# Output weights as the last segment of a four-slot weight ring, and the order of the first output products and the broadcast rows, in a one-core diffusion block

## The reference

```python
p = u @ w_in                       # four branches (conformer, SSD, Hyena, short conv) and gates
merged = sum(gates[b] * (y[b] @ w_branch[b]) for b in "abcd")
mix_lat = merged @ w_out
h_lat = layer_norm(DN_ALPHA * h_lat + mod_lat[2] * mix_lat, ln_g[l, 0], ln_b[l, 0])
ffn_lat = moe_ffn(modulate(h_lat, mod_lat[3], mod_lat[4]), lp)   # h * (1 + scale) + shift
h_lat = layer_norm(DN_ALPHA * h_lat + mod_lat[5] * ffn_lat, ln_g[l, 1], ln_b[l, 1])
```

## Time and profile before

| | |
|---|---|
| median of three runs | 2642.73 us (2639.09 to 2645.9) |
| profiled execution, its own time | 2640.42 us |
| its span | 2638.4 us |
| PE busy | 2436.1 us, 92% |
| DVE busy | 1627.1 us, 62% |
| ACT busy | 941.0 us, 36% |
| PE's granted clock over the span | 0.962 of full speed |

### The profile page before, as it was taken

One profiled execution on the slowest core, in us unless ns is written; L12 is line 12 of the kernel. 1 busy time (PEld: TensorE's weight loads), 2 busy tenths in 40 slices (PEclk: granted clock), 3 DMA queues, 4 the chain that ended last, 5 costly groups with the idle time before them and its releaser, 6 DMA issues. The chain is left out here.

```text
span 2638.4 us, 30395 instructions
## 1 busy us (share of the span) xinstructions
PE 2436.1 (92%) x11864; PEld 1966.6 (75%) x11864; DVE 1627.1 (62%) x1628; ACT 941.0 (36%) x1090; POOL 293.3 (11%) x250
## 2 busy tenths in 40 slices
PE   7889989989997889999999999999499999999984
PEld 3337868768886788788877788878478888888871
DVE  4543359833330773632885635667688888888876
ACT  4132311133321343201111100021267778777763
POOL 3310000000001420000000000100012122121210
PEclk9899989999998999999999999999699999999997
DMA  4341135312323422211111113533579999999946
GB/s 174 129 153 39 42 124 188 136 57 72 114 99 121 128 80 68 96 48 46 48 41 48 40 48 118 202 148 126 239 268 363 368 360 364 365 370 388 386 171 255
DMA packets 95118, 437.49 MB, mean 166 GB/s; under 512 B 16056, under 2 KB 28616, under 8 KB 80298
## 3 DMA queue, kind: packets, MB, share of 16 engines
q1 hardware_dynamic: 68330, 357.81, 36.8%
q0 software_dynamic: 26688, 78.30, 8.5%
HBM read 401.51 MB, written 55.51 MB: 173 GB/s over the span
## 5 line engine op out<-in xcount | busy, mean ns | idle before, releaser
L390 PE MATMUL ps<-uT_upper_rest,ring_rest 128*128 128x512 f32 x1296 | 512.9, 396 | 0.0
L390 PE MATMUL ps<-uT_upper_rest,mix_upper 128*128 128x512 f32 x768 | 307.5, 400 | 9.6 <-DVE mix_val L2329 5.2
L390 PE MATMUL ps<-uT_rest,mix_upper 128*128 128x512 f32 x768 | 306.4, 399 | 0.0
L390 PEld LDWEIGHTS ps<-uT_upper_rest,ring_rest 128*128 128x128 f32 x1296 | 244.6, 189 | 62.2
L390 PEld LDWEIGHTS ps<-uT_upper_rest,mix_upper 128*128 128x128 f32 x768 | 145.5, 190 | 47.4 <-DVE mix_val L2329 5.7
L390 PEld LDWEIGHTS ps<-uT_rest,mix_upper 128*128 128x128 f32 x768 | 145.4, 189 | 33.1 <-issue 0.5
L1762 ACT ACTIVATE mix_gates<-ps 128x1024 f32<-128x1024 f32 x24 | 24.7, 1028 | 385.5 <-PE ps L390 369.0
L1813 DVE TENSOR_TENSOR mix_prod<-mix_gates,ps 128x1024 f32<-128x1024 f32 x24 | 29.3, 1221 | 213.0 <-PE ps L390 213.0
L2793 PE MATMUL ps<-ex_u_raw_rest,uT_rest 128*128 128x256 f32 x560 | 157.1, 281 | 0.0
L390 PE MATMUL ps<-uT_upper_rest,xbc_upper 128*128 128x512 f32 x336 | 136.2, 405 | 7.6 <-DVE ring_rest L819 7.6
L2791 PE MATMUL ps<-ring_rest,uT_rest 128*128 128x256 f32 (+1 forms) x416 | 135.0, 325 | 3.2 <-DVE uT_rest L3100 2.4
(11 more groups left out here) (454 smaller groups left out, 5613.5 us busy)
## 6 DMA issues: line engine op xcount, KB each, us to landing
sb_spare<-in_ex_g SPq DMA_DIRECT2D x35, 2048.0 KB
ex_u_raw<-in_ex_u SPq DMA_DIRECT2D x35, 2048.0 KB, 10.6
sb_merged<-in_ex_d SPq DMA_DIRECT2D x35, 2048.0 KB
ring<-in_conv SPq DMA_DIRECT2D x32, 512.0 KB, 3.3
ring<-in_w_gate SPq DMA_DIRECT2D x32, 512.0 KB, 3.3
mix_piece<-in_w_late POOLq DMA_DIRECT2D x32, 512.0 KB, 5.1
ring<-in_w_ssd SPq DMA_DIRECT2D x21, 512.0 KB, 3.3
ring<-in_w_mod SPq DMA_DIRECT2D x16, 512.0 KB, 3.4
```

The lines of the kernel that those rows point to most:

```text
L390: last = self.nc.tensor.matmul(out, weight, x[:, k, lo:hi], start=(k == 0 and n == 0), stop=(k == kt - 1 and n == 2))
```

## The change

The output weights become the last segment of the ring, with eight items (`ring.claim(KT)`, segment "w_out"). Their first four loads are thus issued in the mixer stage by `Ring.stream`, each as soon as one of merge_d's last four items is used up. The last four are issued in this stage, each when `rest_w_out` has used up the item four places before, and behind the small inputs and the residual tiles 0 and 1 in SP's list. The separate buffer use of `ex_u_raw` and its eight semaphores are gone.

Since the ring's memory holds `w_out` at first, tile 0 of merged's upper part goes to another place (`m_first`, in `uT_rest`), and `cast_merged(1)` waits until all eight items are used up.

On PE project(0) comes first, then the rows of parts 2, 0 and 1 (into banks 2, 4 and 6), then project(1), then the row of part 3 (bank 6), then turn(0). project(2) waits for all four rows to be written back. On ACT the four rows are taken behind the casts, the last of them ahead of the first root. On DVE rest_merged(2) and (3) move behind tile 0's chain, and the chain of tile 0 waits for three rows instead of four.

```diff
+        ring, base = k.ring, k.ring.claim(KT)
...
+        m_first = k.uT_rest[:, 7, :].rearrange("p (k n) -> p k n", n=P)
+        row_order = ((2, 2), (0, 4), (1, 6), (3, 6))
...
             def _(sp):
-                for kt in range(KT):
-                    sp.dma_start(w_out[:, kt, :], a["w_out"][:, kt, :]).then_inc(w_out_in[kt], 16)
                 for dst, src in small:
                     sp.dma_start(dst, src).then_inc(small_in, 16)
                 for t in range(TT):
+                    if t == 2:
+                        ring.stream(sp)
                     if t >= 2:
                         sp.wait_ge(x_used, t - 1)
                     sp.dma_start(x_res[:, t % 2, :], a["x"][t * P:(t + 1) * P, :]).then_inc(x_res_in[t % 2], 16)
...
             def _(pe):
-                for part in range(LATE):
+                def mod_row(part, bank):
                     for h, (lo, hi) in enumerate(HALVES):
-                        mm = nc.tensor.matmul(ps[:, 2 * part + h, :], k.ones[:, :], rows[:, part, lo:hi],
+                        mm = nc.tensor.matmul(ps[:, bank + h, :], k.ones[:, :], rows[:, part, lo:hi],
                                               start=True, stop=True)
                     mm.then_inc(rows_mm, 1)
-                pe.wait_ge(rows_ready, 1)
...
                         if t == 0:
-                            pe.wait_ge(w_split, kt + 1)
+                            pe.wait_ge(ring.freed, ring.done(base + kt))
...
                 for t in range(TT + 2):
                     if t == 1:
+                        pe.wait_ge(rows_ready, 1)
+                    if t == 2:
                         pe.wait_ge(rows_ready, 4)
                         pe.wait_ge(small_in, 64)
                     if t < TT:
                         project(t)
+                    if t == 0:
+                        for part, bank in row_order[:3]:
+                            mod_row(part, bank)
+                    if t == 1:
+                        pe.wait_ge(rows_ready, 3)
+                        mod_row(*row_order[3])
                     if t >= 2:
                         route(t - 2)
                     if 1 <= t <= TT:
...
                 def cast_merged(t):
+                    if t == 1:
+                        act.wait_ge(ring.freed, ring.done(base + KT - 1))
                     if t >= RING:
                         act.wait_ge(mix_mm, t - RING + 1)
...
                 cast_merged(0)
-                cast_w_out(0)
-                mod_row(0)
-                cast_w_out(1)
-                cast_w_out(2)
-                for part in range(1, 4):
-                    mod_row(part)
-                    cast_w_out(part + 2)
-                cast_w_out(6)
-                cast_w_out(7)
-                for t in range(1, RING):
+                for kt in range(KT):
+                    cast_w_out(kt)
+                cast_merged(1)
+                for n in range(3):
+                    take_row(n)
+                for t in range(2, RING):
                     cast_merged(t)
+                take_row(3)
                 for t in range(TT):
                     if t + RING - 1 < TT and t:
                         cast_merged(t + RING - 1)
                     ln.scalar(act, t)
...
                 rest_merged(0)
                 for kt in range(KT):
                     rest_w_out(kt)
-                for t in range(1, RING):
-                    rest_merged(t)
+                rest_merged(1)
                 v.wait_ge(small_in, 64)
-                v.wait_ge(rows_ready, 4)
+                v.wait_ge(rows_ready, 3)
...
                     nc.vector.tensor_tensor(u[:, t, :], s, rows[:, 1, :], ALU.add).then_inc(u_ready, 1)
-                    if 1 <= t and t + RING - 1 < TT:
+                    if t == 0:
+                        rest_merged(2)
+                        rest_merged(3)
+                    elif t + RING - 1 < TT:
                         rest_merged(t + RING - 1)
...
+            ("w_out", KT, lambda j, slot: a["w_out"][:, j * RING + slot, :])]
```

More of the change, by code:

```diff
@@ L2580, in stage_experts @@
         x_lo = k.uT_rest[:, 3, :].rearrange("p (k n) -> p k n", n=P)
-        m_up = k.ring.rest[:, :, :].rearrange("p r (k n) -> p r k n", n=P)
-        w_out_in = [sem(f"w_out_in{kt}") for kt in range(KT)]
-        w_cast, w_split, m_cast, m_split = sem("w_cast"), sem("w_split"), sem("m_cast"), sem("m_split")
+        m_ring = k.ring.rest[:, :, :].rearrange("p r (k n) -> p r k n", n=P)
+        m_first = k.uT_rest[:, 7, :].rearrange("p (k n) -> p k n", n=P)
+        w_cast, m_cast, m_split = sem("w_cast"), sem("m_cast"), sem("m_split")
+        row_order = ((2, 2), (0, 4), (1, 6), (3, 6))
         small_in, x_res_in = sem("small_in"), [sem("x_res_in0"), sem("x_res_in1")]
@@ L2604, in chunk, with m_up @@
             return parts[m // 2][:, b, (m % 2) * HALF:(m % 2 + 1) * HALF]
+        def m_up(t):
+            return m_ring[:, (t - 1) % RING, :, :] if t else m_first
         def slot(m, b):
@@ L2723, in project @@
                         if t == 0:
-                            pe.wait_ge(w_split, kt + 1)
-                        up, lo_part = m_up[:, t % RING, kt, :], merged_rest[:, kt, t * P:(t + 1) * P]
+                            pe.wait_ge(ring.freed, ring.done(base + kt))
+                        up, lo_part = m_up(t)[:, kt, :], merged_rest[:, kt, t * P:(t + 1) * P]
                         for h, (lo, hi) in enumerate(HALVES):
@@ L2836, in _, with take_row @@
             def _(act):
-                def mod_row(part):
-                    act.wait_ge(rows_mm, part + 1)
-                    nc.scalar.activation(rows[:, part, :], ps[:, 2 * part:2 * part + 2, :].rearrange("p b n -> p (b n)"),
+                def take_row(n):
+                    part, bank = row_order[n]
+                    act.wait_ge(rows_mm, n + 1)
+                    nc.scalar.activation(rows[:, part, :], ps[:, bank:bank + 2, :].rearrange("p b n -> p (b n)"),
                                          ACT.Identity, bias=1.0 if part == 2 else 0.0).then_inc(rows_ready, 1)
                 def cast_w_out(kt):
-                    act.wait_ge(w_out_in[kt], 16)
-                    nc.scalar.copy(w_up[:, kt, :], w_out[:, kt, :]).then_inc(w_cast, 1)
+                    ring.arrived(act, base, kt // RING, kt % RING)
+                    nc.scalar.copy(w_up[:, kt, :], ring.buf[:, kt % RING, :]).then_inc(w_cast, 1)
                 def cast_merged(t):
+                    if t == 1:
+                        act.wait_ge(ring.freed, ring.done(base + KT - 1))
                     if t >= RING:
                         act.wait_ge(mix_mm, t - RING + 1)
-                    nc.scalar.copy(m_up[:, t % RING, :, :], merged[:, :, t * P:(t + 1) * P]).then_inc(m_cast, 1)
+                    nc.scalar.copy(m_up(t), merged[:, :, t * P:(t + 1) * P]).then_inc(m_cast, 1)
                 cast_merged(0)
-                cast_w_out(0)
-                mod_row(0)
-                cast_w_out(1)
-                cast_w_out(2)
-                for part in range(1, 4):
-                    mod_row(part)
-                    cast_w_out(part + 2)
-                cast_w_out(6)
-                cast_w_out(7)
-                for t in range(1, RING):
+                for kt in range(KT):
[4 more added lines that the diff above has]
+                for t in range(2, RING):
                     cast_merged(t)
+                take_row(3)
                 for t in range(TT):
@@ L2929, in rest_w_out @@
                     v.wait_ge(w_cast, kt + 1)
-                    nc.vector.tensor_tensor(w_lo[:, kt, :], w_out[:, kt, :], w_up[:, kt, :].bitcast(F32),
-                                            ALU.subtract).then_inc(w_split, 1)
+                    nc.vector.tensor_tensor(w_lo[:, kt, :], ring.buf[:, kt % RING, :], w_up[:, kt, :].bitcast(F32),
+                                            ALU.subtract).then_inc(ring.freed, 1)
                 def rest_merged(t):
@@ L2935, in rest_merged @@
                     cols = slice(t * P, (t + 1) * P)
-                    nc.vector.tensor_tensor(merged_rest[:, :, cols], merged[:, :, cols], m_up[:, t % RING, :, :].bitcast(F32),
+                    nc.vector.tensor_tensor(merged_rest[:, :, cols], merged[:, :, cols], m_up(t).bitcast(F32),
                                             ALU.subtract).then_inc(m_split, 1)
@@ L3258, in weight_segments @@
             whole("w_ssd", 1 + SSD_CONV + SSD_D // P), ("merge_c", 2 * KT - KEPT, merge_c), merge("b", 1),
-            whole("w_conf", 2 * CONF_D // P), whole("w_sc", 3 * SC_D // P), merge("a", 0), merge("d", 3)]
+            whole("w_conf", 2 * CONF_D // P), whole("w_sc", 3 * SC_D // P), merge("a", 0), merge("d", 3),
+            ("w_out", KT, lambda j, slot: a["w_out"][:, j * RING + slot, :])]
 def build_program(nc, a):
@@ L3267, in build_program @@
         k = Kernel(nc, a, ctx)
```

(2 more changed lines are left out.)

1 line of the change is left out of this document (removed).

## The result

| | before | changed |
|---|---|---|
| median | 2640.91 us (2637.28 to 2645.9, four runs) | 2663.64 us (2660.22 to 2667.03, four runs) |
| ratio | | 1.0082, interval 1.0069 to 1.0095 |
| profiled execution, its span | 2640.42, 2638.4 us | 2667.03, 2664.4 us |
| PE, DVE, ACT busy | 2436.1, 1627.1, 941.0 us | 2444.7, 1628.7, 941.5 us |
| PE's granted clock over the span | 0.962 | 0.958 |

The changed kernel is slower by 0.82%, 18 to 25 us by the interval. The forecast of 2657 had the sign and the held root right, but the time is 6.6 us above it and 2.6 us above the upper end of the range. It was added to a median of 2642.73 for the kernel before, which is 2640.91 here; so the increase, forecast at 14.4 us, came out at 21.7 by the ratio.

The account below looks back on a forecast made before the run. TensorE was taken to bound the stage from the first output product on; the start of project(2) moves from 1781.6 to 1796.0, +14.4 us, which on 2642.7 gives 2657 us. The range was 2650 to 2661 us.

Parts of the forecast that it names:

- the held root: Tile 0's root on ScalarE waits behind the fourth row's taking and the table load; TensorE idles 6.8 us before turn(0).
- item 4 split, TensorE goes on: In project(0), TensorE waits for the fifth weight item's split, ready at 1762.8 us, then does four kt of 1.42 us.
- low clock left for project(2): After turn(0) at half clock, the remaining 2.2 us of low clock cost project(2) 1.1 us.
- The wait that is new: Ahead of turn(0): fourth row's taking 1.0, table load 1.28, root 0.2, then VectorE's u 4.0; TensorE idles 6.8 us.
- Rival 1: Tile 0's root isn't held; project(2) waits only for the fourth row's taking: +6.2 us, 2648.9 us, chance 0.07.
- 4: Rival: the change does what it promises, first products 4.8 us earlier and nothing else later: 2638 us, chance 0.03.
- rival 3: Delay is given back behind the projections by something with its own start: at most 14 us, 2643 us, chance 0.04.
- no drain at the table load: At ScalarE's table load before tile 0's root, only 1.28 us counts; a drain would add 1.4 us.
- The last four weight loads: Issued behind small inputs and residual tiles, which need 7.0 us; item 4 lands at 1760.4, item 7 at 1764.2 us.
- rival 2: The last weight loads land later, item 4 needing its own latency behind the residuals: +17 to +20 us, chance 0.13.
- it is hidden in the wait for item 4: The low clock at project(0)'s start, 1.9 us lost, costs nothing since TensorE waits there for the fifth weight item anyway.
- the downstream chain: Work behind the projections starts from tile 7's last product; TensorE has no free time to win the delay back.

Follow-up runs that it names:

- the second pair: The kernel before and the changed kernel, each run and profiled once more, unaltered: 2644.26 us and 2662.91 us, one run each.
- e1: Changed kernel with the fourth row's taking moved behind tile 0's root on ScalarE: 2653.78 us, 1.0046 to the kernel before.
- e5: Kernel before, its early weight loads kept, with the changed kernel's order of rows, products, takings and splits: 2660.26 us, 1.0072 to the kernel before.
- e2: Changed kernel with the last four weight loads issued ahead of the small inputs and residual tiles: 2656.25 us, 1.0058 to the kernel before.
- e7: Changed kernel with only the small inputs moved behind the last four weight loads, residual tiles still ahead: 2655.73 us, 1.0046 to the kernel before.
- e11: The changed kernel once more, unaltered: 2662.91 us, one run.
- e6: e2 with the first row in the mixer's barrier, two rows at the stage's start, the fourth behind route(6): 2642.48 us, 1.0002 to the kernel before.
- e9: e6 with the fourth row ahead of route(6), the small-input wait and the third row's taking later: 2639.78 us, 0.9987 to the kernel before.
- e8: Changed kernel with 26 unused filler matmuls between the fourth row and turn(0): 2659.15 us, 1.0057 to the kernel before.
- e3: Changed kernel with both the edits of e1 and e2: 2648.98 us, 1.0019 to the kernel before.
- e4: Changed kernel's ring loads and SP list, with the kernel before's order of rows and products on all engines: 2645.70 us, 1.0012.

## Why the prediction was right or wrong

The sum's terms, from the start, and what the first pair of profiled executions shows:

| step of the prediction | predicted | measured | difference |
|---|---|---|---|
| item 4 split, TensorE goes on | 13.1 | 15.69 | +2.6 |
| rest of project(0) | 5.7 | 6.99 | +1.3 |
| three rows | 5.0 | 4.75 | -0.2 |
| project(1) | 11.4 | 11.59 | +0.2 |
| fourth row and idle time to turn(0) | 8.4 | 8.54 | +0.1 |
| turn(0) | 1.6 | 1.62 | 0.0 |
| low clock left for project(2) | 1.1 | 1.6 | +0.5 |
| in the stage | +14.4 | +18.9 | +4.5 |
| behind the last product | 0 | +1.5 | +1.5 |

In the second pair the stage's sum is +17.5, and three terms are too low by about the same: item 4 by 1.4, the rest of project(0) by 1.5 (it took 7.24), the part behind the last product by 1.7. (The kernel before's own stretch is 0.7 longer in that pair.) So no one of them alone is the whole miss.

**Right: what bounds the kernel, and the held root.** From project(2) on TensorE works without idle time and the length from there to the last product differs by 1.6, which is the low clock behind the restart, so each delay of its list reached the end. "The wait that is new" was priced by its links and each of them is there. e1 takes out the hold alone and gets 7.7 back; e5 has it without the ring. Rival 1 is out, and so are 3 (the part behind grew) and 4. For rival 3 the prediction named as showing the experts' loads; those rows hold none. In the trace of the kernel before SyncE issues them from 1861.88 on.

**Right: no drain at the table load.** The rows are those of ScalarE above: load until 1798.52, root at 1798.54. By the rule of the Trainium skill, ScalarE: Activation LUTs, section "What ACT_TABLE_LOAD costs", a switch of set would take some 1.4 us more. The trace does not agree with the rule at this place: the taking ahead of the load ends at 1797.22 and the load starts at 1797.24, so there is no room for a drain on either side. (By that rule the forecast would have been 2657 + 1.4 = 2658.4; the prediction has 2658.6.)

**Wrong: "The last four weight loads".** This is the failed step, and the term that was mis-sized is the 7.0 us for small inputs and residual tiles. It had both in at 9.5 from the start, item 4 landing at 10.7 and its split ready at 13.1. The second tile landed at 12.0, so by the prediction's own zero (2.4 from the start) the term was 9.6; the split was ready at 15.69. From the landing to the split it took 2.4, as predicted. I took the 7.0 from tiles that landed at the end of a queue, and treated all bytes in it alike. The shown rates are not alike: the small inputs ran at 215 to 257 GB/s, the others at about 411. By these windows they took some 7 us when they were at the queue's head, and some 5 behind the weights. e2 and e7 show that they, and neither the residual tiles by themselves nor the item's own latency, held item 4: with the tiles ahead and the small inputs behind it is cast at 6.98. So rival 2 had about the right size (+17 to +20) but named the wrong reason; that its size fits is luck. Why the small inputs are slow, many short packets or the copying of one row to all partitions, no run here tells apart. Item 4 also moved by 1.2 between two executions of the same kernel (13.33 and 12.15), so 2.6 is one execution's number; from e11 it is 1.4.

**Wrong: "it is hidden in the wait for item 4".** The low clock of the restart was hidden as predicted. But the wait that hid it was itself 4.11 us without a matmul, and behind it the clock was 0.50 again (0.80 as the mean of the window from 1771). That is the +1.3; in e11 it is 1.5, in e1 2.7. I priced the low clock behind two of three waits. The barrier's 3.95 us in the earlier trace rows with its clock of 0.66 behind it had shown a low clock behind a wait of about this length.

**Wrong: nothing was added behind the last product.** The prediction let "the downstream chain" start from tile 7's last product at its old length. The events looked at behind the last product keep their distance (TensorE's first transpose of an expert comes 55.6 and 55.5 behind it, its first product 59.9 and 59.8), but the clock rises later. Windows of the kernel before, 63.0 to 64.0 behind its last product at 1861.45:

```profile
1924.50:1925.00 0.50, 0.50 (x3) 0.40 (x2) 0.50 (x1) 0.00 (x0) 0.00 (x0) 0.65 0.00 0
1925.00:1925.50 0.50, 0.50 (x4) 0.41 (x3) 0.50 (x1) 0.00 (x0) 0.00 (x0) 1.00 0.00 0
```

Windows of the changed kernel, 64.5 to 66.0 behind its own at 1885.94:

```profile
1950.40:1950.90 0.50, 0.50 (x2) 0.40 (x2) 0.00 (x0) 0.00 (x0) 0.00 (x0) 0.50 0.00 0
1950.90:1951.40 0.50, 0.50 (x2) 0.38 (x2) 0.00 (x0) 0.06 (x1) 0.00 (x0) 0.55 0.00 0
1951.40:1951.90 0.50, 0.50 (x4) 0.40 (x3) 0.00 (x0) 0.50 (x1) 0.00 (x0) 1.00 0.00 0
```

The step from 1.2 to 2.4 GHz is at 63.4 before and at 65.4 after; in the second pair at 63.2 and 65.6. By the first expert's later products that is 0.8 us (1928.60 against 1953.92, 67.15 and 67.98 behind the last product). Where the other 0.7 arises I have not followed. The other kernels, e6 apart, order themselves in the same way: the step is at 62.7 in e9, at 64.6 to 64.8 in e2, e5 and e7, at 65.3 in e8 and at 65.7 to 65.9 in e1, e3 and e4, and the distance to the span's end grows with it, from 776.3 over 777.9 and 778.4 to 778.5 to 778.7. e4 has the 1.8 us without the held root or any move of the rows, and e5 has 1.0 without the ring's loads, so neither half of the change is needed for it. What sets the moment of the step stays open.

**The range.** It ended halfway into rival 2. The loads, the clock and the part behind could all come out longer, and little of the sum could come out shorter: its upper end should have been that rival's own, 2662, plus the runs' scatter.

## What to carry to other kernels

Before work is put into a wait, look at what stands behind it in the other engines' lists: here an early product was paid for with a root that an in-order ScalarE reached only behind the taking of a row that nobody needed yet. Loads ahead in a queue are to be priced by the rate of their own kind, not by their bytes, and every wait that a sum creates is to be checked for its low clock as well. As far as e6 and e9 show, the row matmuls gained only where TensorE's own timeline had idle time with a full clock ahead of it: in the barrier and ahead of route(6), not behind it.

## What the runs showed of the hardware that was not expected

- The four small inputs (1.2 MB) kept the DMA engines 0.68 to 0.74 busy at 215 to 257 GB/s, where weight and residual loads had 411 to 415 GB/s at 1.01 to 1.03.
- A wait of 4.11 us in the middle of full-clock work brought TensorE down to 1.2 GHz, as did waits of 6.67 and 7.52. In e8 one of 2.57 did too: the granted clock was 0.75 in the first 2 us behind it and 0.50 in the next 2. In e6 the barrier's wait of 2.24, with a row ahead of it, left the clock at 1.00.
- What the low clock behind the wait of 6.67 us cost from project(2) to the last product varied: 0.9 to 1.8 in the five executions that had it.
- With the first transpose and the first product of an expert at the same distance from the last product, the clock rose 2.0 to 2.4 us later in the changed kernel than in the one before, in two executions of each.
